# Fewer idle products on TensorE ahead of and inside the v stage, and a later place for one group of modulation columns

## The reference, cut to what matters

```python
c_act = jax.nn.silu(c)
mod = jnp.dot(c_act, w_ada[l]) + b_ada[l]
sh_m, sc_m, g_m, sh_f, sc_f, g_f = jnp.split(mod, N_MOD, axis=-1)
h = modulate(rmsnorm(x, norm_mix_g[l]), sh_m, sc_m)      # h * (1 + sc) + sh
z = jnp.einsum('bsd,de->bse', h, w_in[l])                # u, v, pool, gates
y_a = spatial_gating(jax.nn.gelu(z_sgu), v_norm_g[l], sgu_w[l], sgu_b[l])
...                                                       # pool branch, gates, w_out
x = x + g_f[:, None, :] * grouped_moe(hf, router_w, router_bias, w_exp_gate[l], w_exp_up[l], w_exp_down[l])
return rmsnorm(x, final_norm_g)
```

## Time and profile before

| what | us |
|---|---|
| median of three runs | 771.62 |
| the three runs | 773.86, 770.71, 771.62 |
| the profiled execution | 773.86 |
| its span in the profile | 771.8 |
| mean granted clock of TensorE | 0.987 of full |

### The profile page before, as it was taken

The page is one execution under the profiler, slowest core; times in us unless marked ns, Lnnn a source line. Parts: engine busy times, 40 slices in busy tenths (PEclk is TensorE's granted clock), DMA queues, the critical chain, the costliest instruction groups (busy, mean ns, idle before and its releaser), DMA issues.

```text
span 771.8 us, 10963 instructions
## 1 busy us (share of the span) xinstructions
PE 747.7 (97%) x3500; PEld 616.3 (80%) x3501; DVE 600.1 (78%) x824; ACT 392.4 (51%) x360; POOL 187.7 (24%) x80
## 2 busy tenths in 40 slices
PE   7999999999999999999999998999999999999995
PEld 7888888776888888887788776888888888888884
DVE  5884326855674856668767799999999999999985
ACT  5536324324232231415234575777777677777744
POOL 1000005002000000000062111155555555555533
PEclk9999999999999999999999998999999999999998
DMA  8989314111384654727563637989999999999795
GB/s 304 337 275 382 124 54 164 55 61 50 110 302 133 208 180 159 268 83 259 190 232 123 222 134 275 333 317 397 349 363 373 360 357 380 363 402 359 311 187 167
DMA packets 108708, 187.18 MB, mean 243 GB/s; under 512 B 7095, under 2 KB 58359, under 8 KB 108684
## 3 DMA queue, kind: packets, MB, share of 16 engines
q1 hardware_dynamic: 101276, 173.58, 62.5%
q0 software_dynamic: 5792, 11.65, 5.5%
q10 hardware_dynamic: 1616, 1.65, 0.6%
HBM read 180.47 MB, written 15.73 MB: 254 GB/s over the span
## 4 chain that ended last, share of the span: by engine, by line
PE 85%; DVE 9%; DMA 3%; issue 1%; ACT 1%; SPq 1%; DVEq 0%; POOLq 0%; ACTq 0%
PE ps L1518 25%; PE ps L1519 25%; PE ps L1520 25%; DVE wsplit L842 3%; PE ps L1778 2%; PE ps L1882 1%; PE ps L1648 1%; DMA raw<-in_w_ada 1%; DVE raw L931 1%; PE ps L1709 1%; DMA raw<-in_w_out 1%; PE ps L1814 1%; DMA work<-hf_rows,tok_idx 1%; PE ps L1768 1%; DVE raw L885 1%
## 5 line engine op out<-in xcount | busy, mean ns | idle before, releaser
L842 DVE TENSOR_TENSOR wsplit<-raw,wsplit 128x2048 fp32r<-128x2048 f32 x128 | 290.1, 2290 | 59.4 <-ACT wsplit L565 34.2
L751 ACT ACTIVATE wsplit<-raw 128x2048 fp32r<-128x2048 f32 x96 | 183.8, 1921 | 74.3 <-PE ps L1520 74.0
L512 POOL DMA_INDIRECT expert_rows<-work,dest_now x14 | 100.7, 7190 | 106.2 <-DVE work L1397 98.3
L1518 PE MATMUL ps<-wsplit,hgT 128*128 128x512 f32 x264 | 105.9, 401 | 4.6 <-DVE hgT L1309 4.6
L1519 PE MATMUL ps<-wsplit,hgT 128*128 128x512 f32 x264 | 104.1, 394 | 0.0
L1520 PE MATMUL ps<-wsplit,hgT 128*128 128x512 f32 x264 | 104.1, 394 | 0.0
L1518 PE MATMUL ps<-hT,wsplit 128*128 128x512 f32 x256 | 101.1, 395 | 1.0 <-DVE mx L1027 1.0
L1520 PE MATMUL ps<-hT,wsplit 128*128 128x512 f32 x256 | 99.7, 390 | 0.0
L1519 PE MATMUL ps<-hT,wsplit 128*128 128x512 f32 x256 | 99.7, 389 | 0.0
L885 DVE SCALAR_TENSOR_TENSOR raw<-raw,c_silu 128x256 f32 (+1 forms) x128 | 62.0, 485 | 13.6 <-DMA raw<-in_w_ada 9.6
L1518 PEld LDWEIGHTS ps<-wsplit,hgT 128*128 128x128 f32 x264 | 50.3, 191 | 15.3 <-issue 3.2
(11 more groups left out here) (299 smaller groups left out, 1280.0 us busy)
## 6 DMA issues: line engine op xcount, KB each, us to landing
raw<-in_w_exp_gate SPq DMA_DIRECT2D x32, 1024.0 KB
raw<-in_w_exp_up SPq DMA_DIRECT2D x32, 1024.0 KB
raw<-in_w_exp_down SPq DMA_DIRECT2D x32, 1024.0 KB
raw<-in_w_in SPq DMA_DIRECT2D x20, 1024.0 KB
raw<-in_w_ada SPq DMA_DIRECT2D x16, 1024.0 KB
raw<-in_w_ada SPq DMA_DIRECT2D x16, 512.0 KB, 5.7
expert_rows<-tmp SPq DMA_DIRECT2D x4, 1024.0 KB, 11.3
raw<-in_w_branch_a SPq DMA_DIRECT2D x4, 1024.0 KB
```

The costliest lines, as they stand in the source:

```text
L512: g.indirect_dma_start(out=y_dram, out_offset=bass.IndirectOffsetOnAxis(ap=dest_now[:, 0:1], axis=0), in_=y, in_offset=None, bounds_check= ...
L751: A_(wsplit[:, c, 0, :], raw[:, c, :], ACT.Copy).then_inc(hi_ready, 1)
L842: V.tensor_tensor(wsplit[:, n, 1, :], raw[:, slot, :], wsplit[:, n, 0, :].bitcast(F32), ALU.subtract).then_inc(lo_ready, 1)
L1518: nc.tensor.matmul(out, w_hi, m_hi_, start=first, stop=False)
```

## The change

Three edits, all in TensorE's program. The products ahead of the v stage go from eight to five; `mod_columns(1)` is issued ahead of pair i = 6 rather than i = 4; the wait for `gain_ready` 2 and the five products ahead of quarter 1 go.

```diff
             pe.wait_ge(xT_saved, 1)
             mod_columns(0)
-            idle_products(8, 6, 0)
+            idle_products(5, 6, 0)
...
-                    if k == 1 and i == 4:
+                    if k == 1 and i == 6:
                         mod_columns(1)
                     v_block(0, k, t, half)
             for q in range(1, 4):
...
-                if q == 1:
-                    pe.wait_ge(gain_ready, 2)
-                    idle_products(5, MOD_BANK, P)
                 pe.wait_ge(lo_ready, q + 1)
                 pe.wait_ge(h_lo, 2 * q + 1)
```

## The result

The changed kernel takes 775.14 us in the median of seven runs (774.05 to 777.02), the kernel before 771.41 us in seven runs beside it. By these medians it is slower by 3.7 us or 0.48%. The ratio on record rests on all twenty executions of the changed kernel: 1.0056, with a 95% interval of 1.0040 to 1.0073, or 4.3 us; the bound of 0.5% lies inside the interval. The forecast was 773.7 with a range of 770.1 to 776.3. The time lies where the prediction put the rival of both clock losses (775.3), not its likeliest case.

What follows compares the result with a forecast made beforehand. TensorE's own work was taken as the bound (85% of the time to the end). Late columns (+0.43 us) plus one clock loss (1.6 to 1.7) gave +2.1 on the median of 771.62: 773.7 us, range 770.1 to 776.3.

Steps and rivals of the forecast that it cites:

- the rival of both clock losses: Half clock lasts longer at the v stage and returns in quarter 1: +3.65 us, 775.3 us; chance 0.31.
- its likeliest case: Exactly one of two early clock losses, at the v stage or in quarter 1: +2.1 us, 773.7 us; chance 0.38.
- Edit 3's products overrun by 0.20 us: Ahead of quarter 1: five products end 0.20 us after the input is ready; removing them wins no more.
- +0.43 us without the clock: Start of quarter 1: late columns delay its input, so it starts at 36.67 instead of 36.24.
- the 0.33 taken for the early start: V stage: fewer products ahead let it start 0.42 us earlier at half clock, worth 0.33 us if the clock rises unchanged.
- First place: V stage: a hole of 0.8 us makes half clock last 6.8 us, up to 27.8; +1.62 us, lower bound 0.
- Second place: Ahead of quarter 1: a hole of 2.1 us brings 3.41 us at half clock, costing 1.6 to 1.7 us; lower bound 0.
- its precedents: Falls to half clock at 20.98, after 1.34 us idle, and at 471.5, after most of a 2.95 us wait.
- The last rival: Half-clock stretches at 427 to 430 and 471.5 to 478.4: shifted work wins back 1.3 to 2.7 us, around 769.6; chance 0.13.
- The shift carried to the end: From quarter 2 on: TensorE carries the early delay, counted in full to the end of the kernel.
- the sign of being wrong: Later timeline: the prediction fails if the shift seen at 60 us is gone by 120 us.
- 0.16 for slower by over 0.5%: Whole kernel: chance of slowing by over 3.86 us, 0.13 from both clock losses and 0.03 from other cases.

Runs made afterwards that it cites:

- e4: Changed kernel with eight products kept ahead of the v stage; columns late, none ahead of quarter 1; 1.0021 of the kernel before, +1.7 us.
- e6: Changed kernel with seven instead of five products ahead of the v stage; 1.0032 of the kernel before, +2.5 us.
- e1: Kernel before with only the products ahead of the v stage cut from eight to five; ratio 1.0012, +0.5 us.
- e5: Changed kernel with the wait for `gain_ready` 2 and the five products ahead of quarter 1 put back; 1.0030 of the kernel before, +2.3 us.
- e7: Changed kernel with the wait for `gain_ready` 2 and nine products ahead of quarter 1; 1.0026 of the kernel before, +2.1 us.
- e9: The changed kernel unaltered, timed once more; 1.0050 of the kernel before, +4.2 us.
- e2: Kernel before with only the columns of quarter 1 moved from ahead of pair 4 to pair 6; ratio 1.0003, +0.7 us.
- e3: Kernel before without the wait for `gain_ready` 2 and the five products ahead of quarter 1; ratio 0.9986, -0.8 us.
- e10: Second run of the kernel before without the wait and the five products ahead of quarter 1; ratio 1.0003, +0.3 us.
- e8: Kernel before with seven products ahead of the v stage, columns at pair 4, and no wait or products ahead of quarter 1; ratio 0.9998, -0.3 us.
- e11: Kernel before without wait and products ahead of quarter 1, plus two products ahead of the columns of quarter 0; ratio 1.0000, -0.2 us.

## Why the prediction was right, and where it was not

- *Edit 3's products overrun by 0.20 us, and without the late columns that is all they cost:* right, 0.21 and 0.18.
- *The columns of quarter 1 become the late input; +0.43 us without the clock:* right in mechanism, and 0.2 too small. With eight products ahead the lateness alone is 0.76 (e4), and with seven, which start the v stage as early as five do, it is 0.62 (e6), so of the 0.33 taken for the early start 0.14 was found (in e6 the half clock also reached 0.9 us into the v products and in e4 it ended before them, so this is rough). The 0.33 was a slip in the count: at 24.57 the changed kernel begins its third product and the one before its second, one product ahead, which is worth 0.227.
- *First place, priced +1.62:* the mechanism is right. Quarter 1 was +2.06 late against +2.05 forecast, but this sum does not contain the 0.33, which drops out of it (0.76 + 1.29). Against the 0.62 measured in e6 the long stretch itself cost 1.44, not 1.62. The hole was smaller than the 0.8 forecast: 0.36 as printed, 0.56 by the distance of starts, and it sufficed. The order of events came as foreseen, with the columns of quarter 1 14.56 us after those of quarter 0 (34.5 - 19.95 = 14.55 forecast) and VectorE idle in front of them. With five products ahead the long stretch came in five of five profiles (changed, e1, e5, e7, e9), with seven or eight in one of eight (e2). The cleanest pair is e4 against e5; in e1 and e2 the half clock set in 1.0 us before the one-column products ended, and without these two it is four of four against none of seven. Not foreseen was that the long stretch also comes without a hole, when the half clock sets in during the one-column products (e2): the median of edit 1 alone (+0.5) may be below its profile (+0.9) because the kernel before pays at times too. That last is argued, not shown; the time taken away by the clock, +1.8 in e1, has a standard error of 0.7 and does not settle it.
- *Second place, priced 1.6 to 1.7:* right. The shift grows by 1.36 us from quarter 1 to the columns of quarter 2, as quarter 1 began 0.45 us into the stretch; where quarter 1 had the whole stretch before it (e4, e6, e9) it grows by 1.55 to 1.59. A hole of 2.0 us brought the fall in four of four profiles (changed, e4, e6, e9); holes of 0.66 to 0.91 us or none, in none of nine. e7 filled the hole, and the fall went. The length of a hole alone is no rule, though: later in the changed kernel holes of 1.93 us (to 437.15) and 2.91 us (to 475.31) passed at full clock, while e4 fell at 436.95, behind a hole of 1.94 us. And the fall at 427.1 in the kernel before, which the prediction did not count among its precedents, came with no hole over 0.44 us in the 3.4 us ahead of it, with products of 2, 64 and 80 columns among the others. What decides between such cases stays open.
- *The choice among the cases:* here the forecast failed. I gave exactly one loss 0.38 and both 0.31. Early in the kernel both, with the lateness, cost 3.42 us (+3.65 forecast for that case); two comparisons measured 3.7 and 4.2. The rows had pointed at both places, and I discounted each for lack of precedents as if a miss in either were likely. The measured time lies inside the range of the forecast only because the range was drawn to hold the case of both losses.
- *The last rival (the later stretches come or go):* the mechanism is real, but it hits the kernel before as well and gave the change nothing in the median. It is what made the two profiled times equal, by 2.9 us at 471.5 (3.1 forecast) and by nothing at 427 (1.7 forecast), where a wait for a transfer took up what the clock gave back.
- *The shift carried to the end:* right up to 472.14 (3.0 to 3.2 us at every row), so the sign of being wrong, a shift gone by 120 us, did not come.
- *0.16 for slower by over 0.5%:* too low for a ratio of +0.56% whose interval (0.40 to 0.73%) holds the bound; it follows from the same discount.

No version was clearly faster than the kernel before. e3 with e10, e8 and e11 all lie within 0.14% of it.

## What to carry to other kernels

Products that nobody reads can hold up TensorE's clock over a wait: before taking them out, compare the hole that remains with holes in the same trace that did and did not bring the clock down, and price 3.4 us at half clock, about 1.6 us where TensorE is at work throughout and nothing where it then waits for a transfer anyway. Work that feeds another engine (here 1 us of columns) belongs at the moment its input is ready; two blocks later it made that engine late and so opened the very hole. And two profiled executions can agree while the medians differ by 4 us: compare early stretches row by row, and take the total from many runs.

## What the runs showed that I had not expected

The first half-clock stretch lasted 3.4 or 6.8 us in all profiles and nothing between; with every product in place it was 6.8 once, when it set in 1.0 us before the one-column products ended (e2). The later half-clock stretches near 430 and 475 us come and go between executions of one kernel. The one near 430 moved little, since TensorE waits for a transfer behind it; the one near 475 lasted 6.8, 3.4 or 0 us, and its absence was worth 2.9 us, more than any one of the edits.
